# A hybrid attention/SSM/expert kernel: the scaling of two groups of attention scores moves within VectorE's program

## The reference

```python
ya = s5_mixer(ua, ...)        # 256 channels: a linear state recurrence, then gelu and a gate
yb = rms_unit(moba_mixer(qb, kb, vb, ...))   # 8 heads of causal softmax attention over 256 tokens
yc = retention_mixer(qc, kc, vc, gc, ...)    # 4 heads of decayed linear attention
y = concatenate([ya, yb, yc]) * mix_out_g
x = x + y @ w_out
x = x + peer_layer(rms_norm(x), ...)         # 16384 experts, top 16 for each of 8 heads
```

## Time and profile before

| | us |
|---|---|
| median of 3 runs | 990.34 (989.86 to 990.83) |
| the profiled execution, its own time | 990.89 |
| its span in the trace | 989.0 |
| PE busy | 925.8 (94%) |
| DVE busy | 734.6 (74%) |
| ACT busy | 529.0 (53%) |
| POOL busy | 464.1 (47%) |

### The profile page before, as it was taken

How to read it: one execution, slowest core, us unless ns; L and a number is a source line. 1 busy time by engine, 2 the same in 40 slices (tenths; PEclk the granted TensorE clock), 3 DMA queues, 4 the chain that set the end, 5 groups by cost and what they waited for, 6 DMA issues and landing times.

```text
span 989.0 us, 20056 instructions
## 1 busy us (share of the span) xinstructions
PE 925.8 (94%) x5888; PEld 828.0 (84%) x5888; DVE 734.6 (74%) x1591; ACT 529.0 (53%) x1042; POOL 464.1 (47%) x370
## 2 busy tenths in 40 slices
PE   7679399999979889999999999999999999999998
PEld 7546168899979889999999999988888888888886
DVE  5999944203999930388888888688888888888886
ACT  7333075555544445555555555665556666566653
POOL 4668406587999998877777777500000000000000
PEclk8789799999999999999999999999999999999999
DMA  9424022315556556656556556677767767776773
GB/s 341 155 86 155 16 85 75 118 55 202 197 186 210 183 199 215 210 198 202 196 189 205 191 190 202 202 252 237 250 237 243 241 237 245 235 245 238 246 240 134
DMA packets 67436, 191.39 MB, mean 194 GB/s; under 512 B 6480, under 2 KB 8272, under 8 KB 67408
## 3 DMA queue, kind: packets, MB, share of 16 engines
q1 hardware_dynamic: 67408, 191.04, 57.0%
HBM read 173.71 MB, written 17.30 MB: 193 GB/s over the span
## 4 chain that ended last, share of the span: by engine, by line
PE 66%; POOL 11%; DVE 10%; issue 8%; ACT 3%; DMA 1%; POOLq 0%; SPq 0%; DVEq 0%; ACTq 0%
PE ps L423 21%; PE ps L425 20%; PE ps L424 20%; POOL w_lo L1462 10%; DVE routing L731 4%; PE ps L660 3%; DVE routing L876 2%; DVE small L731 1%; PE ps L405 1%; DVE route_t L731 1%; DMA routing<-in_w_in 1%; DVE raw L731 1%; ACT w_hi L1168 1%; ACT h_hi L1175 0%; POOL w_lo L1426 0%
## 5 line engine op out<-in xcount | busy, mean ns | idle before, releaser
L1462 POOL TENSOR_TENSOR w_lo<-raw,w_hi 128x512 fp32r<-128x512 f32 x256 | 345.6, 1372 | 79.2 <-ACT w_hi L1318 78.8
L1318 ACT ACTIVATE w_hi<-raw 128x512 fp32r<-128x512 f32 x512 | 308.3, 628 | 132.2 <-PE ps L425 131.3
L423 PE MATMUL ps<-h_hi,w_hi 128*128 128x256 f32 x1088 | 309.6, 285 | 16.5 <-POOL w_lo L1462 15.2
L424 PE MATMUL ps<-h_lo,w_hi 128*128 128x256 f32 x1088 | 307.8, 283 | 0.0
L425 PE MATMUL ps<-h_hi,w_lo 128*128 128x256 f32 x1088 | 307.8, 283 | 0.0
L423 PEld LDWEIGHTS ps<-h_hi,w_hi 128*128 128x128 f32 x1088 | 208.7, 192 | 19.4 <-POOL w_lo L1462 17.4
L731 DVE TENSOR_TENSOR w_lo<-raw,w_hi 128x512 fp32r<-128x512 f32 x256 | 177.4, 693 | 52.5 <-ACT w_hi L1318 41.1
L424 PEld LDWEIGHTS ps<-h_lo,w_hi 128*128 128x128 f32 x1088 | 208.8, 192 | 0.0
L425 PEld LDWEIGHTS ps<-h_hi,w_lo 128*128 128x128 f32 x1088 | 208.8, 192 | 0.0
L423 PE MATMUL ps<-w_hi,hot_gate 128*128 128x512 f32 x512 | 199.2, 389 | 0.0
L424 PE MATMUL ps<-w_lo,hot_gate 128*128 128x512 f32 x512 | 199.2, 389 | 0.0
(11 more groups left out here) (195 smaller groups left out, 914.9 us busy)
## 6 DMA issues: line engine op xcount, KB each, us to landing
raw<-in_u_t SPq DMA_DIRECT2D x128, 512.0 KB, 3.3
raw<-in_v SPq DMA_DIRECT2D x128, 512.0 KB, 3.3
act_spill<-acts SPq DMA_DIRECT2D x62, 256.0 KB, 2.1
acts<-act_spill SPq DMA_DIRECT2D x62, 256.0 KB, 3.4
routing<-in_w_in SPq DMA_DIRECT2D x5, 2048.0 KB, 11.4
routing<-in_w_out SPq DMA_DIRECT2D x2, 2048.0 KB, 8.4
routing<-in_w_q SPq DMA_DIRECT2D x2, 2048.0 KB, 8.0
xs<-in_x SPq DMA_DIRECT2D x2, 512.0 KB, 4.0
```

Source lines behind the costliest of these rows:

```text
L423: pe.matmul(dst, s_hi, m_hi, start=first and i == 0, stop=False)
L424: pe.matmul(dst, s_hi, m_lo, start=False, stop=False)
L1318: A.activation(w_hi[:, 2 * (s % 2) + h, :], raw[:, s, h * HALF:(h + 1) * HALF], ACT.Copy)\
L1462: G.tensor_tensor(w_lo[:, slot, :], raw[:, s, h * HALF:(h + 1) * HALF], w_hi[:, slot, :].bitcast(F32), ALU.subtract).then_inc(lo_ready, 1)
```

## The change

DVE's program is put in another order. The scaling, masking and maxima of the first score group (L914, L917) come ahead of `rotate_back(0)`; those of the second group (L921, L929) come between `rotate_back(0)` and `rotate_back(1)`. The sign change (L909) and the signal `states_ready` stay behind `rotate_back(1)`, and so now stand behind both score groups. No operation is added or removed, and no wait is added; the programs of the other engines are untouched.

```diff
             dve.wait_ge(consts_in, 80)
-            rotate_back(0)
-            rotate_back(1)
-            V.tensor_scalar(c_s[:, 1], c_s[:, 1], -1.0, None, ALU.mult).then_inc(states_ready, 1)
-            dve.wait_ge(states_ready, 1)
-
             dve.wait_ge(s_psum, 1)
             s1_ = ps[:, 4:8, :].rearrange("p b (h k) -> p (b h) k", h=2)
             V.scalar_tensor_tensor(att1, s1_, SCALE, mask_s.unsqueeze(1).to_broadcast([P, MH, S]), ALU.mult,
                                    ALU.add).then_inc(s_read, 1)
             dve.wait_ge(s_read, 1)
             V.tensor_reduce(hmax[:, 8:16], att1, AX.X, ALU.max, negate=True).then_inc(max_ready, 1)
+            rotate_back(0)
             dve.wait_ge(s_psum, 2)
             dve.wait_ge(ret_rot_ready, 1)
             for b in range(2):
@@ -928,6 +924,9 @@
             dve.wait_ge(s_read, 2)
             V.tensor_reduce(hmax[:, 0:8].rearrange("p (t g) -> p t g", t=TT), att0, AX.X, ALU.max,
                             negate=True).then_inc(max_ready, 1)
+            rotate_back(1)
+            V.tensor_scalar(c_s[:, 1], c_s[:, 1], -1.0, None, ALU.mult).then_inc(states_ready, 1)
+            dve.wait_ge(states_ready, 1)
 
             dve.wait_ge(y_psum, 1)
             for c in range(S5_C):
```

## The result

| | us |
|---|---|
| before, median of 4 runs | 990.23 (989.86 to 990.83) |
| changed, median of 4 runs | 983.8 (982.96 to 984.13) |
| ratio, with its 95% interval | 0.9933 (0.9916 to 0.995) |
| changed, the profiled execution, its own time | 984.13 |
| its span | 982.4 |

Four of the later runs, three of edited kernels and one of the kernel before, took 1172 to 1845 us instead of about 1000; every median, range and ratio here is of the other runs.

A forecast was written before the change was run, and what follows sets the result against it. DVE alone was taken to set the pace from 100 to 120 us, with PE work in series. Lead 8.64 less 2.4 for the clock saves 6.2: 990.89 to 984.7, less 0.55 gives 984.1 us; range 981.5 to 987.4.

The forecast's parts named there:

- What bounds the stage: From 100 to 120 us DVE alone sets the pace; 10.9 us of PE work waits in series for L914's reading.
- the lead: Start of L515, behind the states: forecast at 123.39 instead of 132.03 us, 8.64 us earlier.
- No contention for L914 and L917: On DVE beside POOL's rotation: both keep their undisturbed times, L914 2.32 us and L917 2.21 us.
- POOL's rotation out of the way, one operation still met: POOL ends at about 106.5 us, not 111.4; one turn-back operation meets it, 0.43 us more, so `rotate_back(0)` takes 7.69.
- PE's replay: PE before the states: L506 follows at 104.29 without a gap, 1.2 us, projection 7.13, ending at about 112.6.
- The price of the low clock: L515 to ACT's L1257, after PE's idle gap: 5.33 us instead of 2.96, 2.4 more.
- rival (a): At L515: the low clock costs nothing, pace set by issue or weight loads; 981.7 us, chance 0.12.
- The factor 1.8: Assumed slowdown of L515 and L524 at the low clock, from rows showing 1.85 and 1.70.
- The rest shifts as a whole: From the end of L524 on, the steps stay the same, only shifted, 6.2 us earlier.
- (b): On PE after L524: the clock rises late, after gate product L556, costing 2.5 us; 986.6 us, chance 0.10.
- (d): On PE, L563 to L596: the clock stays low until the mixer ends; 4.0 us slower, 994.3 us, chance 0.03.
- (c): On DVE: L914, L917 and `rotate_back(0)` still contend with POOL, costing 0.8 and 2.6 us; 987.5 us, chance 0.06.

## Why the prediction was right

*What bounds the stage*: right. Ahead of L515 stood PE work that waited for a reading on DVE, and with it off the chain the lead is 9.22 us against 8.64 forecast. The forecast's lead holds 10.9 us of PE's work, less 4.8 of DVE's, plus 2.6 from contention; the runs without the rotation confirm both parts, the order with 3.5 net of the clock and contention with 2.5 to 2.9.

*No contention for L914 and L917*: right, 2.29 us both, beside POOL operations of 0.72 to 0.74. The Trainium skill, page "SBUF — State Buffer", section "Who interferes with whom", has the same: a DVE instruction with at most one SBUF input, outside the modes that use two ports, does not contend with GpSimd. The same page of the Trainium skill has the engine that comes second block for the whole of the other's instruction. That fits no better now than in the prediction: in the trace of before, turn-back and POOL operations ran side by side at 1.64 and 1.66 us from start to start, less than the sum of their undisturbed prices, 1.2 and 0.7.

*POOL's rotation out of the way, one operation still met*: wrong in the changed kernel's profile. `rotate_back(0)` took 9.68 us, not 7.69. The step that failed was the starting point: it was taken as fixed at 100.98, with POOL at 96.69. In this execution PE's transposes of queries and keys (L488) met the low clock, the projection after them was late, and with it POOL. The scans then had DVE to themselves for longer: 7.05 us instead of 9.16, and L909 began 2.53 earlier. The three rows are of the kernel before, of the changed one, and of the changed one without the rotation:

```profile
87.89 1.94 PE L488 MATMUL ps<-con,routing 128*128 128x128 f32 x16 [1.63 <-POOL routing L1414]
87.31 3.49 PE L488 MATMUL ps<-con,routing 128*128 128x128 f32 x16 [2.09 <-POOL routing L1413]
87.83 1.94 PE L488 MATMUL ps<-con,routing 128*128 128x128 f32 x16 [2.53 <-POOL routing L1413]
```

I had also read 0.84 us as POOL's undisturbed price beside the scans. It is 0.72, and the scans contend too: 0.80 us from one to the next beside POOL and 0.375 alone, by their starts in the trace of before. So the one operation still met did not come either: in the run with PE's work moved ahead POOL was done at 105.70, not 106.5, and `rotate_back(0)` took 7.2. The two errors, -2.53 for the start and +1.99 for the turn-back, nearly cancel, and as that run shows, this is no accident: POOL's rotation meets DVE once, in the one place or the other. The forecast had not argued it, so here the number came right where the place was wrong. It also left out that L914, once first, waits for L497; that cost 0.27 here.

*PE's replay*: right. L506 follows without a gap, 8.2 us for both, ended by 113.5.

*The price of the low clock*: right in place and nearly in size, 2.64 against 2.4. L515 took 3.66 against 1.97, a factor 1.86, so its pace follows the granted clock; rival (a) falls. The Trainium skill's rule on the spacing at the two clocks ("TensorE: Matmul & The Clock Gate", section "Wait — 56ns, not 53.3ns?") would have given, as an estimate, up to 5.9 us, twice the 2.96. The factor 1.8 gave 5.33; the measured 5.60 lies between.

*The rest shifts as a whole*: right, 835.0 and 834.9 us after the mixer. The clock rose at 128.5, so rivals (b) and (d) did not come; (c), that the turn-back still meets POOL, came in half, but with the scans relieved in its place. Its price was added up wrongly: of the 2.6 for `rotate_back(0)` the forecast had 0.43 in it already, and L917 was given none of the 0.8 that L914 got. The two nearly cancel.

## What to carry to other kernels

When an engine works through a long stretch alone, look at what stands behind it in its own order and put first what releases another engine; the price is what the moved work delays, here 4.8 us of DVE against 10.9 of PE. Moving the wait moves PE's idle gap too, and the small matmuls behind it then run at half the clock: count that before claiming the lead. A cover for such a gap has to reach nearly to its end: one that stopped 3.5 us short was worth nothing by the median, one that stopped 1.2 us short kept the clock.

## What was not expected of the hardware

The clock fell between 2.1 and 5.3 us after PE's end: 2.1 in the changed kernel without the rotation, 2.7 in the kernel before with 60 products, 4.7 in the changed kernel, 5.3 in the kernel before. The length of a gap alone does not decide: ahead of L488, 2.09 us of idleness were followed by the low clock in the changed kernel (it fell at 87.5), and 2.53 us were not in the one without the rotation.

The clock came back between 3.0 us (only the first group moved) and 5.7 us (the changed kernel) after PE's return, so the price of the same gap differs: from the start of L515 to ACT's first copy it was 2.6 us in the changed kernel and 1.9 without the rotation.

Scans on DVE contend with tensor operations on POOL, although they read one tile of 128 x 128 and small ones: 0.80 against 0.375 us a scan.
